# One shared order of attention items, latent branch first, with weight splits, top-k rounds and transposes listed between, and packed small inputs

## What is computed

```python
(q_a, k_a, v_a, q_i, k_i, w_i, q_b, k_b, v_b, c_q, c_kv, k_r) = jnp.split(h @ w_in, splits, axis=-1)
o_a = dsa_attention(q_a, k_a, v_a, q_i, k_i, w_i)      # 4 heads over the 64 keys of the highest index score
o_b = diff_attention(q_b, k_b, v_b, lam, lam_init, subln)   # 4 heads, two softmax maps subtracted
q_c = (rms_norm(c_q, q_norm) @ w_uq).reshape(b, s, 8, 96)   # latent branch (MLA), 8 heads
kv = (rms_norm(c_kv, kv_norm) @ w_ukv).reshape(b, s, 8, 128)
o_c = mla_attention(q_nope, q_rope, k_nope, k_rope, v_c)
return jnp.concatenate([o_a, o_b, o_c], axis=-1) @ w_out
```

## Time and profile before

| | |
|---|---|
| median of 3 runs | 1678.57 us (1674.35 to 1679.5) |
| profiled execution | 1676.76 us, its span 1675.0 us |
| PE busy | 1596.9 us, 95% |
| DVE busy | 1271.3 us, 76% |
| ACT busy | 1034.2 us, 62% |
| POOL busy | 61.1 us, 4% |
| mean granted clock of TensorE | 0.947 |
| HBM read | 429.30 MB, 257 GB/s |

### The profile page before, as it was taken

One profiled execution on the slowest core, in us unless ns is written; L12 is line 12 of the kernel. 1 busy time (PEld: TensorE's weight loads), 2 busy tenths in 40 slices (PEclk: granted clock), 3 DMA queues, 4 the chain that ended last, 5 costly groups with the idle time before them and its releaser, 6 DMA issues.

```text
span 1675.0 us, 20863 instructions
## 1 busy us (share of the span) xinstructions
PE 1596.9 (95%) x7246; PEld 1296.6 (77%) x7246; DVE 1271.3 (76%) x1562; ACT 1034.2 (62%) x1320; POOL 61.1 (4%) x128
## 2 busy tenths in 40 slices
PE   6979999999898998999999999999999999999996
PEld 5857788888686677888888888888888888888885
DVE  4676555555547646989989989989989989989995
ACT  4334354444334335778778778778778778778774
POOL 1400000000032000000000000000000000000000
PEclk9965999999898578999999999999999999999999
DMA  8311265455251024999999999999989999999992
GB/s 270 132 51 51 101 219 199 166 188 179 82 181 65 1 102 165 369 335 358 352 338 357 349 336 363 351 326 367 350 326 366 350 327 365 351 328 359 358 362 104
DMA packets 184456, 431.10 MB, mean 257 GB/s; under 512 B 6352, under 2 KB 13008, under 8 KB 184400
## 3 DMA queue, kind: packets, MB, share of 16 engines
q1 hardware_dynamic: 180272, 427.11, 70.2%
q10 hardware_dynamic: 4128, 3.25, 0.6%
HBM read 429.30 MB, written 1.05 MB: 257 GB/s over the span
## 4 chain that ended last, share of the span: by engine, by line
PE 89%; DVE 5%; ACT 3%; issue 2%; DMA 1%; DVEq 0%; POOL 0%; SPq 0%
PE pair L765 47%; PE work L765 32%; PE work L741 3%; PE work L984 2%; PE pair L741 2%; PE pair L823 1%; PE work L752 1%; PE work L893 1%; ACT w_hi L1085 1%; ACT arena L1216 1%; DMA ring<-in_w_in 1%; DVE nmax L1475 1%; DVE w_lo L1388 0%; DVE arena L1566 0%; PE work L998 0%
## 5 line engine op out<-in xcount | busy, mean ns | idle before, releaser
L1388 DVE TENSOR_TENSOR w_lo<-ring,w_hi 128x1024 fp32r<-128x1024 f32 (+2 forms) x812 | 968.7, 1214 | 254.4 <-ACT w_hi L1085 248.6
L1085 ACT ACTIVATE w_hi<-ring 128x1024 fp32r<-128x1024 f32 (+2 forms) x812 | 849.4, 1054 | 350.0 <-PE pair L765 186.6
L765 PE MATMUL pair<-w_hi,hnT_hi 128*128 128x512 f32 x1120 | 448.5, 400 | 5.1 <-DVE hnT_lo L1396 3.0
L765 PE MATMUL pair<-w_lo,hnT_hi 128*128 128x512 f32 x1120 | 442.6, 395 | 0.0
L765 PE MATMUL pair<-w_hi,hnT_lo 128*128 128x512 f32 x1120 | 442.5, 395 | 0.0
L765 PEld LDWEIGHTS pair<-w_hi,hnT_hi 128*128 128x128 f32 x1120 | 210.5, 188 | 53.5 <-DVE hnT_lo L1396 3.6
L765 PEld LDWEIGHTS pair<-w_hi,hnT_lo 128*128 128x128 f32 x1120 | 210.4, 188 | 50.9
L765 PEld LDWEIGHTS pair<-w_lo,hnT_hi 128*128 128x128 f32 x1120 | 210.6, 188 | 47.6
L765 PE MATMUL work<-w_hi,hidT_hi 128*128 128x512 f32 x552 | 219.7, 398 | 2.6 <-DVE hidT_lo L1634 1.4
L765 PE MATMUL work<-w_lo,hidT_hi 128*128 128x512 f32 x552 | 218.3, 395 | 0.0
L765 PE MATMUL work<-w_hi,hidT_lo 128*128 128x512 f32 x552 | 218.3, 395 | 0.0
(11 more groups left out here) (177 smaller groups left out, 1111.1 us busy)
## 6 DMA issues: line engine op xcount, KB each, us to landing
ring<-in_moe_w_gate SPq DMA_DIRECT2D x56, 2048.0 KB, 8.1
ring<-in_moe_w_up SPq DMA_DIRECT2D x56, 2048.0 KB, 8.5
ring<-in_moe_w_down SPq DMA_DIRECT2D x56, 2048.0 KB, 7.9
ring<-in_dense_w_gate SPq DMA_DIRECT2D x7, 2048.0 KB, 7.8
ring<-in_dense_w_up SPq DMA_DIRECT2D x7, 2048.0 KB, 7.7
ring<-in_dense_w_down SPq DMA_DIRECT2D x7, 2048.0 KB, 7.6
ring<-in_w_in SPq DMA_DIRECT2D x4, 2048.0 KB, 8.1
ring<-in_w_out SPq DMA_DIRECT2D x4, 2048.0 KB, 8.0
```

The lines of the kernel that those rows point to most:

```text
L765: mm = pe.matmul(b, lhs[x_part][k + kk], w[w_part][:, kk, :], start=(first and kk == 0 and i == 0), stop=(last and kk == 1 and i == 2))
L1085: return act.activation(o, i, ACT.Copy)
L1388: dve.tensor_tensor(lo, raw, hi.bitcast(F32), ALU.subtract).then_inc(lo_done, 1)
```

## The change

`attention_order` no longer computes the list: it reads it from a string. Layer 1 takes the same list with another opening. Splits (SP n), top-k rounds (TK t r), the latent means (C1) and the angles (AN) are items of it; `SPLIT_AT` and the queue of rounds are gone.

```diff
+ATTENTION = """
+N1.0 N1.1 N2.0 N2.1 X.0.0 X.0.1 SP.0 SP.1 SP.2 SP.3 X.1.0 X.1.1 SP.4 PC.0 C1.0 AN SP.5 SP.6 PC.1 C1.1 SP.7
+PA.0 C2.0 CT.0 SP.8 SP.9 KV.0.1 C2.1 PA.1 QC.0.0 CT.1 KV.0.0 SP.10 QC.0.1 SP.11 PB.0 MQ.0.1 MK.0.0 MK.0.1
+MQ.0.0 QC.1.1 KV.1.1 QC.1.0 SP.12 KV.1.0 SP.13 PB.1 U.0 MQ.1.0 MK.1.1 SP.14 SP.15 MK.1.0 SP.16 SP.17 U.1
+SP.18 MQ.1.1 CB.0 TP.0 PI.1 SP.19 PI.0 PK.0 U.2 CB.1 TP.1 PK.1 O.0 U.3 CB.2 TP.2 CB.3 O.1 U.4 IT.0 U.5 TP.3
+U.6 O.2 CB.4 TP.4 U.7 CB.5 KIT.0 O.3 O.4 TP.5 U.8 BT.0 CB.6 CB.8 TP.6 O.5 KIT.1 CB.7 U.9 TP.7 O.6 O.7 IT.1
+CB.9 TP.9 U.10 O.9 TP.8 U.11 CB.11 U.12 O.8 TP.11 CB.10 TP.10 O.11 U.13 TK.0.0 O.10 TK.0.1 CB.12 U.14 TP.12
+TK.0.2 CB.13 CB.14 TK.0.3 U.15 TK.0.4 TP.13 BT.1 TK.0.5 O.12 O.13 TK.0.6 TP.14 CB.15 TK.0.7 U.16 SP.20 TP.15
+SP.21 U.17 AT.1 AT.0 O.14 SP.22 TK.1.0 U.18 TK.1.1 CB.16 CB.17 TK.1.2 TP.16 SP.23 TK.1.3 CB.18 U.19 TP.17
+TK.1.4 U.20 CB.19 TP.18 U.21 O.18 CB.20 TP.19 TK.1.5 SP.24 U.22 O.19 TP.20 CB.21 D1.0 U.23 O.17 O.20 TP.21
+TK.1.6 SP.25 D2.0 O.21 SP.26 U.24 CB.22 CB.23 OT.0.0 O.15 OT.0.1 CB.24 O.16 TP.22 U.25 TK.1.7 TP.23 CB.25
+WO.0.0 U.26 O.22 SP.27 O.23 TP.24 U.27 CB.26 WO.0.1 O.24 TP.25 O.25 TP.26 CB.27 TP.27 D1.1 O.26 NF1.0 D2.1
+O.27 NF2.0 OT.1.1 OT.1.0 XF.0.0 WO.1.0 WO.1.1 NF1.1 NF2.1 SP.28 SP.29 SP.30 XF.0.1
+"""
+    if layer == 1:
+        opening = order.index(("X", 1, 1)) + 1
+        rest = [item for item in order[opening:] if item != ("AN",)]
+        first = [[("N1", t), ("N2", t), ("X", t, 0), ("X", t, 1)] for t in range(2)]
+        split = [item for item in order[:opening] if item[0] == "SP"]
+        order = first[0] + first[1][:2] + split + first[1][2:] + [item for item in rest if item not in first[1]]
+        order.append(("SP", 31))
...
-    PROJ = {"PC": (c_q, end), "PI": (q_i, k_i), "PK": (k_i, k_b), "PA": (q_a, q_i), "PB": (k_b, c_q)}
+    PROJ = {"PC": (c_q, end), "PA": (q_a, q_i), "PB": (k_b, c_q), "PI": (q_i, k_i), "PK": (k_i, k_b)}
+    LOADS = ("PC", "PA", "UP", "PB", "PI", "PK", "WO0", "WO1")
...
+    UNITS = [("mla", t, p) for t in range(T) for p in range(HC // 2)]
+    UNITS += [("idx", t, p) for t in range(T) for p in range(IDXP)]
+    UNITS[12:12] = [("diff", 0, p) for p in range(2)]
+    UNITS += [("diff", 0, p) for p in range(2, HB)]
+    UNITS += [("dsa", 0, p) for p in range(HA // 2)] + [("diff", 1, p) for p in range(HB)]
+    UNITS += [("dsa", 1, p) for p in range(HA // 2)]
...
+        order[:] = [item for item in order if not (item[0] in ("CB", "TP", "O") and item[1] in INDEX)]
...
+        def in_extra(part):
+            return isinstance(part, int) and part - LAYER_PARTS + 1 in LAYER_PART
...
-                    key = (layer, name, T - 1) if name in PROJ else (layer, "WO", T - 1, int(name[2]))
-                    eng.wait_ge(job_done, JOB[key] + 1)
+                    keys = [(layer, name, t) if name in PROJ else (layer, "WO", t, int(name[2])) for t in range(T)]
+                    eng.wait_ge(job_done, max(JOB[key] for key in keys) + 1)
...
-                    if (layer, c) == (0, "PI"):
-                        sp.wait_ge(loaded_small, 16 * 6)
...
-                        if (layer, t) == (0, 0):
+                        if (layer, t) == (0, 1):
                             act.wait_ge(angles_ready, 1)
                             act.activation(sin[:, :, :], ang, ACT.Sin).then_inc(trig_ready, 1)
...
-                    elif name == "TP" and UNITS[item[1]][0] != "mla":
+                    elif name == "TP":
...
-            load_gain(a["attn_norm"][0])
-            act.dma_start(freq[:, :], row(a["rope_freq"], NF)).then_inc(loaded_small, 16)
-            for i, name in enumerate(("q1", "k1", "q2", "k2")):
-                v = a[f"diff_lambda_{name}"]
-                act.dma_start(lamv[:, :, i, :], v.unsqueeze(0).to_broadcast([P, DEPTH, DB])).then_inc(loaded_small, 16)
+            load_gain(("attn", 0))
+            act.dma_start(setup, a["setup"]).then_inc(loaded_small, 16)
             load_layer_gains(0)
```

More of the change, by code:

```diff
@@ L31 @@
 PARTS = 7
+EXTRA_AT = 896 + 1536 + 1536 + 1600 + 1024 + 1024 + 768 + 256 + 1024
 WBANKS = 4
[L35 to L78, removed]
@@ new lines, with attention_order @@
+WO.0.0 U.26 O.22 SP.27 O.23 TP.24 U.27 CB.26 WO.0.1 O.24 TP.25 O.25 TP.26 CB.27 TP.27 D1.1 O.26 NF1.0 D2.1
+O.27 NF2.0 OT.1.1 OT.1.0 XF.0.0 WO.1.0 WO.1.1 NF1.1 NF2.1 SP.28 SP.29 SP.30 XF.0.1
+"""
+def attention_order(layer):
+    words = [word.split(".") for word in ATTENTION.split()]
+    order = [(name, *map(int, numbers)) for name, *numbers in words]
+    if layer == 1:
[5 more added lines that the diff above has]
+        order.append(("SP", 31))
@@ L147, in hybrid_block @@
     for layer in range(DEPTH):
-        for c in PROJ:
-            USE[(layer, c)] = len(USE)
-        for name in ("UP", "WO0", "WO1"):
+        for name in LOADS:
             USE[(layer, name)] = len(USE)
@@ L1061, in _ @@
                     emptied(pe, (1, "XF", t, i))
-                product(b, E, [hnT[:, k, tile(t)] for k in range(KT)], [router[:, k, :] for k in range(KT)]) \
+                product(b, E, [hnT[:, k, tile(t)] for k in range(KT)], [router[:, k * E:(k + 1) * E] for k in range(KT)]) \
                     .then_inc(job_done, 1)
@@ L1114, in split_hi @@
                     arrived(act, use, rounds)
-                if part >= PARTS:
+                if part >= PARTS and not in_extra(part):
                     part_free(act, part - PARTS, shift)
@@ L1224, in attention @@
                             .then_inc(out_of(key), 1)
-                    if item in SPLIT_AT[layer]:
-                        first, final = SPLIT_AT[layer][item]
-                        for n in range(first, final + 1):
-                            split_hi(LAYER_PART[layer] + n)
+                    elif name == "SP":
+                        split_hi(LAYER_PART[layer] + item[1])
             def silu(half, step, t, used):
@@ L1552, in attention @@
                             index_unit(layer, n)
-                            if UNITS[n][2] == IDXP - 1:
-                                rounds += [(UNITS[n][1], r) for r in range(TOPK // 8)]
                         else:
@@ L1615, in attention @@
                             dve.sem_inc(residual_ready, 1)
-                    elif item == ("PC", 0) and layer == 0:
+                    elif name == "AN":
                         angles()
-                    if item in SPLIT_AT[layer]:
-                        first, final = SPLIT_AT[layer][item]
-                        for n in range(first, final + 1):
-                            split_lo(LAYER_PART[layer] + n)
-                    if rounds and name in ("TP", "O"):
-                        select_round(*rounds.pop(0))
-                assert not rounds
+                    elif name == "SP":
+                        split_lo(LAYER_PART[layer] + item[1])
+                    elif name == "TK":
+                        select_round(item[1], item[2])
             def hidden(half, step, t, used):
```

200 lines of the change are left out of this document (104 added, 96 removed).

## The result

| | before | changed |
|---|---|---|
| median of the runs beside each other | 1678.81 us | 1680.24 us |
| profiled execution, its span | 1676.76, 1675.0 us | 1682.36, 1680.6 us |
| PE busy | 1596.9 us | 1583.5 us |
| mean granted clock | 0.947 | 0.957 |

The ratio is 1.0018, with a 95% interval of 1.001 to 1.0025: 0.2% slower, inside the 0.3% that I called no change. 1680.0 was forecast. TensorE is busy 13 us less, mostly since it runs less at 1.2 GHz, but it idles 19 us more, and the time didn't fall: gains and losses cancel, and the experiments had to find which.

What follows compares the result with a forecast made beforehand. TensorE bounds the first and last part of attention, VectorE the middle, TensorE at half clock the latent units. Layer 0 -0.8 and layer 1 +2.2 sum to +1.4 us on 1678.6: 1680.0 forecast, range 1662 to 1707.

Steps and rivals of the forecast that it cites:

- The start: Layer 0's beginning: first weights land at 13.5 us instead of 15.8, 2.3 us gained once, bounds 0 and 4.
- the packing: Small inputs at the start: ten ScalarE-queue DMAs become three, SP no longer waits for them; 2.3 us gain.
- Projections: Layer 0, from 15.5 us: 66.3 us of TensorE work with three latent units, plus 7.8 of stalls, ending at 89.6.
- The stall behind the table loads: Layer 0 projections: trigonometry's two table loads ahead of split 7 make TensorE wait about 3.0 us.
- Latent units warm: Latent units of tile 1, index units of tile 0: 20.4 us with TensorE at full clock; the other end 33.
- The rival with the cold units: Latent units: TensorE falls to 1.2 GHz after the projections in both layers, 13 us more each, 1706; chance 0.27.
- Middle and tail: Attention behind the latent units: 15.0 us, 28.1 to tile 0's output projection, 24.4 to tile 1's, which takes 11.2.
- The ends: Behind the output projection: splits and XF half delay what follows; 5.2 us given back in layer 0, 8.0 in layer 1.
- Layer 1's opening: Layer 1's start: norm and X of tile 1 come ahead of the splits, so PC starts 2.5 us later than 451.29.
- The experts and the dense steps: Dense layer and experts: same instructions, weights loaded no later, so no term in the sum.
- The ends are cheaper: Middle stalls and half of the 5.2 and 8.0 us don't appear: 7 us less per layer, 1665.5; shared chance 0.25.
- More stalls in the projections: Projections: ScalarE and VectorE wait together at splits for freed buffers, 5 us per layer, 1690; chance 0.13.

Runs made afterwards that it cites:

- the pause: Changed kernel with TensorE made to wait on five GpSimd multiplications behind PK.1 in layer 0, ahead of the latent units: 1699.82 us, ratio 1.0133.
- The mended end: Changed kernel with splits 28 to 30 beside the output projection and the second XF half right behind the first, both layers: 1668.8 us, ratio 0.9946.
- the 64 bytes: Changed kernel with one unused tensor of 64 bytes per partition, moving the split weights back to their former addresses: 1675.47 us, ratio 0.9986.
- one pair of pauses: Changed kernel, TensorE paused in layer 0 behind PK.1 (1699.82 us, ratio 1.0133) or between TP.0 and PI.1, ahead of weight products (1690.45 us, ratio 1.0075).

## Why the prediction was right in its number, and where not in its reasons

**The start.** Forecast: first product at 15.5; measured 15.14. The first weights were there near 13 us, as said (issued at 1.7, 11.0 us to landing). But the term was sized by the weights, and now x, norm and transposes end last. All 2.8 us of the packing's gain came.

**Projections.** Forecast 74.1 us from the first product to the end of PK; measured 70.7 (15.14 to 85.9). The stall behind the table loads (2.5 us of idling) and the cold products behind it came as described. TensorE idled 3.5 us in all, where 4.3 were booked; most of the rest is work that was booked too high.

**Latent units warm.** Forecast 20.4 us, measured 20.9, at 1.00. The rival with the cold units is out, and the pause priced it: some 15 us a layer, not 13. The deciding point was named rightly, the state at entry.

**Middle and tail.** Index units and top-k 15.0 (measured 14.9), to output projection 28.1 (29.0), the tail 24.4 (24.6), products 11.2 (11.45). The output projection ended at 187.1, not 189.7: 8.6 us gained, not 6.0. In layer 1 at 619.9, not 623.4.

**The ends.** Given back in layer 0: 6.0 us (forecast 5.2); RT of tile 1 18.1 us behind the projection (18.2), 7.9 lost (8.0). The mended end returned 12 us of these 14. This was the term that decided the sum, and it was right. Behind RT the sum has nothing, and the profile shows 32.1 us from RT's end to the first turn of the experts instead of 29.4. That isn't a term left out: with the same order and the 64 bytes it took 29.2, so it differs between executions.

**Layer 1's opening.** Forecast 2.5 us later, measured 1.6, although the dense layer ended 1.6 us earlier: the opening itself takes 3.2 us more. The forecast started layer 1 from the kernel before and left out the 0.8 us gained in layer 0. Behind the first product the projections took 65.2 us instead of the 69.6 forecast.

**The step that failed:** "The experts and the dense steps are the same instructions, with their weights loaded no later." They are the same instructions at other addresses. That cost 5.4 us by ratio, and without it the changed kernel is at 0.9986, 2.4 us faster than the one before. My sum for the order was too high by about 4 us (the projections took 3.4 us less than forecast in layer 0 and 4.4 in layer 1), and a term of 5 us was missing. The two errors cancelled: that the number stood is luck, while the account of the stages isn't.

**Rivals.** "The ends are cheaper" fell: they cost what was said, and the order's gain without the address term is 2.4 us, not 14. "More stalls in the projections" fell too.

## What to carry to other kernels

When a list moves work behind the last product of a stage, count all of it as exposed, on every engine in order. Before a few us in one profiled execution are put down to the change, look at the same instructions in other executions. Where TensorE has to wait, put the wait ahead of long weight products rather than ahead of a mix like the latent units: one pair of pauses priced that at 3 against 15 us. And when an edit adds or drops a tensor, compare the pitch of the untouched inner loop before any reason is given for a difference: 64 bytes moved it by 0.4%, and 32 more by 2.5%.

## What the runs showed of the hardware

The time of a weight product depends on where its buffers start in on-chip memory: 24 of 128x512 in 5.62, 5.60 or 5.44 to 5.49 us, same instructions, clock 1.00, TensorE busy throughout. The Trainium skill ("SBUF — State Buffer", Operand start alignment) asks only for a start at a multiple of the element's size and says that this is about legality and not speed; all three places are legal, and the measurement shows that they differ in speed.

The clock has a memory of the work: the same mix of logits, transposes and 64-wide products stood at 1.00 for 20 us when it began there, and at 0.50 for 35 us when a pause of 4.0 us had come first. Another mix of logits and transposes, entered at 0.50, was back near 1.00 within 7 us.

The clock's way back isn't the same in every execution: behind identical instructions in layer 1, 72 weight products took 17.1 us in six executions and 18.2 to 18.7 in three.
